# Sparse attention in pairs of heads, the convolution norm under the query columns, and conv units of w_out in one PSUM region

## The chip, the cores and the metric

The kernel runs on one core of a Trainium2 chip. The metric is the device time of one execution in microseconds.

## What is computed

Two transformer blocks in float32 over 256 tokens of width 2048. The change touches the first block's mixer: native sparse attention (16 query heads of 64, 4 key/value heads; three branches: compressed blocks, selected blocks, window) beside a conformer convolution, both closed by one projection `w_out`. With 256 tokens the selection takes all four blocks and the window reaches everything, so those two branches are causal attention over all keys.

```python
proj = rms_norm(x, mix_norm_g) @ w_in                    # q, kv, gate_logits, conv_in
# per query head: three causal softmaxes
p_cmp = masked_softmax(q_s @ k_cmp.T + bias_c, valid_c)  # 15 compressed keys
p_sel = masked_softmax(q_s @ k_slc.T + bias_s, valid_s)  # 256 keys
p_win = masked_softmax(q_s @ k_win.T + bias_w, valid_w)  # 256 keys
attn = g0 * (p_cmp @ v_cmp) + g1 * (p_sel @ v_slc) + g2 * (p_win @ v_win)
# convolution branch
u = causal_depthwise_conv(a * sigmoid(gate), conv_w, conv_b)
conv = silu(layer_norm(u, conv_ln_g, conv_ln_b))
x = x + concatenate([attn, conv], -1) @ w_out
```

Behind it come a gated FFN with convolution, then a second block (latent attention and differential attention, gated mix, FFN) and a final norm.

## The kernel before, in words

Activations lie transposed, features on partitions and the 256 tokens in the free dimension. Each large product splits its operands in a high part (fp32r) and a low remainder: `hp`/`yp` hold for each k-tile 256 high and 256 low columns, and each weight tile is brought by SP's queue into `w_raw`, rounded by ScalarE into `w_hi` (`hi`, L531) and its remainder made by GpSimd (until the q columns) or VectorE in `w_lo` (`lo`, L849). Four slots of such weight units rotate. `unit` (L1507 to L1520) is the matmul form: per k-tile one matmul of `w_hi` with 512 columns (high and low of the activation, into the two halves of a PSUM bank) and one of `w_lo` with the 256 high columns; the two halves are added by VectorE when it takes the bank.

The order of work on every engine is written out by hand and tied together with semaphores. `free` waits until VectorE has taken so many chunks, `used` until PE has finished so many units.

After the q columns of w_in (four groups g, each four units, taken by VectorE at L865) the stage of the change begins:

- The convolution's layer norm. PE sums `conv_y` after q group 0 and its squares after q group 2 (`sums`, L1592). VectorE centres it (L1120), forms the variance (L1128), and after the last q group refines the root (L976 to L979), scales (L1130) and applies gain and bias (L1132, eight ops). ScalarE makes the root and a sigmoid (L644); VectorE gates (L1186), ScalarE copies the high half (L676), VectorE makes the low half (L1190, "mixed").
- Attention, head by head. PE: `scores(h)` (L1712 to L1716, 64 partitions as contraction, the head's half of the array's rows), into banks 2+2s and 3+2s with s = h % 3. VectorE: `scores` (L1147 bias and scale, L1149 to L1152 maxima). ScalarE: `exps` (L652). VectorE: `weighted` (L1159 to L1163, one over the sum times the gate, applied to all segments). PE: `turns` (L1505, eight transposes). ScalarE: `turned` (L659 to L661, copies to ptA, ptB). PE: `values` (L1738 to L1743, 64 output partitions, the head's half of the array's columns, bank 1). Every second head: ScalarE `y_hi` (L666), VectorE `y_lo` (L1169).
- Under it, one conv unit of w_out a head from head 2 on (`conv_unit`): the eight k-tiles of the convolution rows for one 128-column tile of w_out, into bank 0 (the last into bank 4); VectorE's `conv_out` adds the bank's two halves to x (L1176, L1177). Its weights go through `hi` and `lo` like all others.

PE's loop before is, for head h: scores(h+1), turns(h-1), conv_unit(h-2), values(h-1). After the last head the product `w_out` over the attention rows begins (`gemm`).

## Time and profile before

| | before |
|---|---|
| median of 3 runs | 3037.05 us (3034.68 to 3042.62) |
| the profiled execution | 3043.87 us |
| its span | 3041.9 us |
| PE busy | 2947.5 us (97%) |
| DVE busy | 2118.6 us (70%) |
| ACT busy | 1371.4 us (45%) |
| mean granted clock of PE | 0.975 |
| DMA | 507.34 MB, 167 GB/s |

A PE row is one engine pass; an fp32 matmul is two passes with a weight load each. PEld is the weight load, which may overlap PE. The granted clock is in parts of 2.4 GHz (1.0 and 0.5 are its two levels). Times in the views are microseconds from the span's start, and the bracket at a row's end is how long the engine stood idle ahead of it and what ended that.

### The profile page before, as it was taken

The page shows a single profiled execution, that of the slowest core. Times are in us where ns is not written, and L with a number is a line of the kernel's source. Part 1 is how long each engine was busy: PE and PEld are TensorE (multiplying, and loading weights), DVE is VectorE, ACT ScalarE, POOL GpSimd, SP SyncE. Part 2 cuts the span into 40 slices and gives each one's busy share as a digit, 9 for nine tenths or more (in the row PEclk, how much of TensorE's full clock was granted, in tenths as well). Part 3 has the DMA queues.
Part 4 walks back from the last instruction along what each step waited for, and adds up shares of the span by engine and source line. Part 5 has one row for each costly group of instructions (what it writes and reads, how often), then busy time and mean ns, then how long its engine had stood idle before and what let it go on. Part 6 is the DMA issues. An engine that isn't in the chain of part 4 may idle for free.

```text
span 3041.9 us, 49637 instructions
## 1 busy us (share of the span) xinstructions
PE 2947.5 (97%) x16944; PEld 2562.0 (84%) x16944; DVE 2118.6 (70%) x3202; ACT 1371.4 (45%) x1786; POOL 172.4 (6%) x81
## 2 busy tenths in 40 slices
PE   7998999999999999969999999999999999999998
PEld 5877788888888888958878888888888888888887
DVE  4974777885887687557776777777756766675674
ACT  4324555653454455324444455454345543343444
POOL 4864000000000000000000000000000000000000
PEclk9998899999999999889999999999999999999998
DMA  9655135655555565435445655555555655656553
GB/s 229 177 139 120 58 91 166 192 183 190 184 187 188 187 190 166 128 99 143 141 142 182 178 172 165 172 172 174 187 164 175 196 191 184 196 178 201 181 181 123
DMA packets 596729, 507.34 MB, mean 167 GB/s; under 512 B 90123, under 2 KB 594715, under 8 KB 596251
## 3 DMA queue, kind: packets, MB, share of 16 engines
q1 hardware_dynamic: 595040, 503.61, 54.9%
q0 software_dynamic: 560, 2.12, 0.2%
q8 instruction: 53, 0.87, 0.1%
q10 hardware_dynamic: 1035, 0.40, 0.1%
q14 instruction: 41, 0.34, 0.0%
HBM read 503.88 MB, written 2.12 MB: 166 GB/s over the span
## 4 chain that ended last, share of the span: by engine, by line
PE 91%; DVE 6%; issue 1%; ACT 1%; DMA 0%; DVEq 0%; SPq 0%; ACTq 0%
PE banks L1518 55%; PE banks L1519 28%; PE banks L1573 2%; PE banks L1505 1%; DVE arena L865 1%; DVE w_lo L849 1%; DVE banks L1043 1%; PE banks L1592 1%; PE banks L1712 0%; PE banks L1832 0%; DMA cst<-tables 0%; PE banks L1879 0%; PE banks L1738 0%; PE banks L1835 0%; PE banks L1600 0%
## 5 line engine op out<-in xcount | busy, mean ns | idle before, releaser
L1518 PE MATMUL banks<-hp,w_hi 128*128 128x512 f32 x4416 | 1573.8, 400 | 24.3 <-issue 10.0
L531 ACT ACTIVATE w_hi<-w_raw 128x1024 fp32r<-128x1024 f32 (+2 forms) x960 | 996.9, 1045 | 1212.2 <-PE banks L1519 1206.1
L849 DVE TENSOR_TENSOR w_lo<-w_raw,w_hi 128x1024 fp32r<-128x1024 f32 (+2 forms) x889 | 1062.0, 1205 | 565.7 <-ACT w_hi L531 548.6
L1519 PE MATMUL banks<-hp,w_lo 128*128 128x256 f32 x4416 | 1241.9, 281 | 0.0
L1518 PEld LDWEIGHTS banks<-hp,w_hi 128*128 128x128 f32 x4416 | 835.8, 189 | 226.5 <-issue 18.5
L1518 PE MATMUL banks<-yp,w_hi 128*128 128x512 f32 x2880 | 1014.8, 397 | 2.7 <-DVE yp L1267 2.6
L1519 PEld LDWEIGHTS banks<-hp,w_lo 128*128 128x128 f32 x4416 | 840.8, 190 | 2.4 <-issue 1.9
L1519 PE MATMUL banks<-yp,w_lo 128*128 128x256 f32 x2880 | 808.3, 281 | 0.0
L1518 PEld LDWEIGHTS banks<-yp,w_hi 128*128 128x128 f32 x2880 | 543.3, 189 | 128.8 <-DVE yp L1267 3.6
L1519 PEld LDWEIGHTS banks<-yp,w_lo 128*128 128x128 f32 x2880 | 547.1, 190 | 0.1
L865 DVE TENSOR_REDUCE arena<-banks 128x256 f32<-128x512 f32 (+1 forms) x392 | 251.3, 683 | 120.1 <-PE banks L1519 119.8
L834 POOL TENSOR_TENSOR w_lo<-w_raw,w_hi 128x1024 fp32r<-128x1024 f32 x71 | 170.1, 2399 | 82.5 <-ACT w_hi L531 82.2
L1518 PE MATMUL banks<-arena_r,w_hi 128*128 128x512 f32 x272 | 100.0, 407 | 15.4 <-DVE w_lo L849 15.1
L1043 DVE SCALAR_TENSOR_TENSOR banks<-arena,vec,banks 128x256 f32<-128x256 f32 x232 | 102.0, 485 | 3.7
L966 DVE TENSOR_TENSOR arena<-arena,cst 128x512 f32<-128x512 f32 x133 | 91.9, 691 | 4.3
L1239 DVE SCALAR_TENSOR_TENSOR arena<-arena,vec 128x256 f32<-128x256 f32 x176 | 77.5, 481 | 17.1 <-ACT arena L704 11.2
L1519 PE MATMUL banks<-arena_r,w_lo 128*128 128x256 f32 x272 | 77.1, 284 | 0.0
L1518 PEld LDWEIGHTS banks<-arena_r,w_hi 128*128 128x128 f32 x272 | 52.0, 191 | 29.0 <-issue 15.1
L704 ACT ACTIVATE arena<-arena,vec 128x256 f32<-128x256 f32 x88 | 48.2, 595 | 51.2 <-DVE arena L966 51.2
L1212 DVE TENSOR_TENSOR x<-banks,x 128x256 f32<-128x256 f32 (+1 forms) x128 | 53.1, 415 | 20.5 <-PE banks L1519 20.5
L694 ACT ACTIVATE arena<-arena 128x512 f32<-128x512 f32 x44 | 27.8, 633 | 80.6 <-DVE arena L966 61.4
L762 ACT ACTIVATE arena<-arena,small 128x128 f32<-128x128 f32 x64 | 28.7, 449 | 76.9 <-DVE small L1352 76.9
(234 smaller groups left out, 1489.9 us busy)
## 6 DMA issues: line engine op xcount, KB each, us to landing
w_raw<-in_w_in SPq DMA_DIRECT2D x480, 256.0 KB, 3.0
w_raw<-in_w_up SPq DMA_DIRECT2D x352, 256.0 KB, 2.9
w_raw<-in_w_ffn_up SPq DMA_DIRECT2D x176, 256.0 KB, 3.7
w_raw<-in_w_ffn_gate SPq DMA_DIRECT2D x176, 256.0 KB, 3.0
w_raw<-in_w_down SPq DMA_DIRECT2D x160, 256.0 KB, 3.0
w_raw<-in_w_ffn_down SPq DMA_DIRECT2D x160, 256.0 KB, 3.0
w_raw<-in_w_out SPq DMA_DIRECT2D x128, 256.0 KB, 3.2
w_raw<-in_w_mla_proj SPq DMA_DIRECT2D x64, 256.0 KB, 3.0
```

The lines of the kernel that those rows point to most:

```text
L531: nc.scalar.activation(w_hi[:, s, 0:n], w_raw[:, s, 0:n], ACT.Copy).then_inc(hi_ready, 1)
L704: ins = nc.scalar.activation(dst[:, c, :], buf[:, c, FTAPS - 1:], ACT.Identity, scale=vdyn("ffn_conv_w", ch + (FTAPS - 1) * 2 * FT), bias= ...
L834: nc.gpsimd.tensor_tensor(w_lo[:, s, 0:n], w_raw[:, s, 0:n], w_hi[:, s, 0:n].bitcast(f32), ALU.subtract)\
L849: v.tensor_tensor(w_lo[:, s, 0:n], w_raw[:, s, 0:n], w_hi[:, s, 0:n].bitcast(f32), ALU.subtract)\
L865: v.tensor_reduce(dst, pair(b)[0:rows], X, ALU.add).then_inc(chunk_out, 1)
L966: return v.tensor_tensor(dst, dst, bcast(r_row, 2), ALU.mult)
L1043: ins = v.scalar_tensor_tensor(conv_y[:, t, :] if k == TAPS - 1 else acc, src, w, acc, ALU.mult, ALU.add)
L1212: link(v.tensor_tensor(xt, banks[:, c, 0:T], xt, ALU.add))
L1239: ins = v.scalar_tensor_tensor(dst[:, c, :], buf[:, c, k:k + T], vdyn("ffn_conv_w", at_ch[c] + k * 2 * FT), dst[:, c, :], ALU.mult, ALU.add)
L1518: mm(banks[:, b, :], w_hi[:, s, at:at + P], rhs[:, kt, :], start=kt == kt_first, stop=False)
L1519: ins = mm(banks[:, b, 0:T], w_lo[:, s, at:at + P], rhs[:, kt, 0:T], start=False, stop=kt == kt_last)
L1573: ins = mm(banks[:, STAT, at + b:at + b + 1], src[:, t, b * P:(b + 1) * P], ones[:, 0:1], start=False, stop=t == KT - 1, skip_group_check= ...
```

## The change

1. The norm of the convolution: its second sums go after q group 1; VectorE's refinement, scaling and affine follow there, gate and low half behind q group 2; ScalarE's root, sigmoid and high copy are placed between its q high halves.
2. Heads go in pairs. `scores(n)` on PE interleaves the two heads of a pair matmul by matmul (one in array rows 0 to 63, one in 64 to 127); `values(n)` interleaves them too (output partitions 0 to 63 and 64 to 127, both in bank 1). PE's loop is, for pair n: turns(2n), conv_unit(2n), scores(n+1), turns(2n+1), conv_unit(2n+1), values(n). Conv units start with head 0.
3. A conv unit (`folded`) accumulates its three products in one region of 256 columns: per k-tile `w_hi` with the high half, `w_hi` with the low half, `w_lo` with the high half, all 256 columns, in half n % 2 of bank 0. `conv_out` is one add.

```diff
@@ -637,12 +635,15 @@
     nc.scalar.activation(gtok, gtok, ACT.Sigmoid).then_inc(sem("gates_sigmoid"), 1)
     act.wait_ge(sem("conv_centred"), 1)
     nc.scalar.activation(conv_sq, conv_y, ACT.Square).then_inc(sem("conv_squares"), 1)
-    his("q", 0, 8, 16)
+    his("q", 0, 8, 12)
     root(ROOT["conv"], nv_conv)
-    his("w_out_conv", 0, 0, 2)
+    his("q", 0, 12, 14)
     act.wait_ge(sem("conv_affine"), 1)
     nc.scalar.activation(conv_sq, conv_y, ACT.Sigmoid).then_inc(sem("conv_sigmoid"), 1)
-    his("w_out_conv", 0, 2, 4)
+    his("q", 0, 14, 16)
+    act.wait_ge(sem("conv_gated"), 1)
+    nc.scalar.activation(yp[:, CT:KT, 0:T], conv_y, ACT.Copy).then_inc(sem("conv_hi"), 1)
+    his("w_out_conv", 0, 0, 4)
     def exps(h):
@@ -665,22 +666,25 @@
         act.wait_ge(sem("nsa_pv"), n + 1)
         nc.scalar.activation(yp[:, n, 0:T], banks[:, 1, 0:T], ACT.Copy).then_inc(sem("nsa_hi"), 1)
-    for h in range(NQ):
...
+    def next_hi(n):
+        if n < 12:
+            hi("w_out_conv", 0, n + 4)
+        else:
+            hi("w_out", 0, n - 12)
+    exps(0)
+    exps(1)
+    for n in range(NQ // 2):
+        turned(2 * n)
+        next_hi(2 * n)
+        if n:
+            y_hi(n - 1)
+        turned(2 * n + 1)
+        if n < NQ // 2 - 1:
+            exps(2 * n + 2)
+            exps(2 * n + 3)
+        next_hi(2 * n + 1)
     y_hi(NQ // 2 - 1)
-    his("w_out", 0, 2, 4)
     closing("w_out")
     tiny_root(ROOT[1], tiny(0), tiny(1))
@@ -1123,14 +1127,19 @@
             dve.wait_ge(sem("gates_sigmoid"), 1)
             g0 = gtok[:, 0, :].rearrange("p (h r) -> p h r", r=NBR)[:, :, 0]
             link(v.tensor_scalar(g0, g0, c_("sees"), None, ALU.mult))
-        if g == 2:
             dve.wait_ge(sem("conv_sum"), 2)
             v.tensor_scalar(nv_conv[:, 0, :], banks[:, 7, T:], 1.0 / CCH, EPS, ALU.mult, ALU.add).then_inc(sem("variance"), 1)
-    refine(ROOT["conv"], nv_conv)
...
+            refine(ROOT["conv"], nv_conv)
+            link(v.tensor_tensor(conv_y, conv_y, bcast(nv_conv[:, 2, :], CT), ALU.mult))
+            for t in range(CT):
+                ins = v.tensor_scalar(conv_y[:, t, :], conv_y[:, t, :], vcol("conv_ln_g", t), vcol("conv_ln_b", t),
+                                      ALU.mult, ALU.add)
+            ins.then_inc(sem("conv_affine"), 1)
+        if g == 2:
+            dve.wait_ge(sem("conv_sigmoid"), 1)
+            v.tensor_tensor(conv_y, conv_y, conv_sq, ALU.mult).then_inc(sem("conv_gated"), 1)
+            dve.wait_ge(sem("conv_hi"), 1)
+            v.tensor_tensor(yp[:, CT:KT, T:], conv_y, yp[:, CT:KT, 0:T].bitcast(f32), ALU.subtract).then_inc(sem("mixed"), 1)
     def scores(h):
@@ -1172,38 +1181,34 @@
     def conv_out(n):
         used("w_out_conv", 0, n + 1)
-        b = CONV_BANK.get(n, 0)
...
+        v.tensor_tensor(x[:, n, :], banks[:, 0, n % 2 * T:(n % 2 + 1) * T], x[:, n, :], ALU.add).then_inc(chunk_out, 1)
+    def next_lo(n):
+        if n < 12:
+            lo("w_out_conv", 0, n + 4)
+        else:
+            lo("w_out", 0, n - 12)
+    scores(0)
+    scores(1)
+    lows("w_out_conv", 0, 0, 4)
+    weighted(0)
+    weighted(1)
+    for n in range(NQ // 2):
+        conv_out(2 * n)
+        if n < NQ // 2 - 1:
+            scores(2 * n + 2)
+            scores(2 * n + 3)
+        if n:
+            y_lo(n - 1)
+        next_lo(2 * n)
+        if n < NQ // 2 - 1:
+            weighted(2 * n + 2)
+        conv_out(2 * n + 1)
+        next_lo(2 * n + 1)
+        if n < NQ // 2 - 1:
+            weighted(2 * n + 3)
+    y_lo(NQ // 2 - 1)
     def residual(c0):
         def run(i):
@@ -1504,6 +1509,17 @@
         return nc.tensor.transpose(dst, src, ident[0:rows, 0:rows])
+    def folded(ph, j, k0, ku, o, rhs, kt_last):
+        s, r = slot_of(ph, j)
+        pe.wait_ge(lo_ready[s], r + 2)
+        for k in range(ku):
+            kt, wh, wl = k0 + k, w_hi[:, s, k * P:(k + 1) * P], w_lo[:, s, k * P:(k + 1) * P]
+            mm(o, wh, rhs[:, kt, 0:T], start=k == 0, stop=False)
+            mm(o, wh, rhs[:, kt, T:], start=False, stop=False)
+            ins = mm(o, wl, rhs[:, kt, 0:T], start=False, stop=kt == kt_last)
+        ins.then_inc(unit_used, 1)
     def unit(ph, i, j, k0, ku, cols, where, rhs, kt_last, operand=None, kt_first=0):
@@ -1697,23 +1713,26 @@
             ins.then_inc(sem("gates_turned"), 1)
             pe.wait_ge(sem("conv_done"), 1)
             sums(banks[:, 7, 0:T], conv_y, CT).then_inc(sem("conv_sum"), 1)
-        if g == 2:
+        if g == 1:
             pe.wait_ge(sem("conv_squares"), 1)
             sums(banks[:, 7, T:], conv_sq, CT).then_inc(sem("conv_sum"), 1)
-    def scores(h):
...
+    def scores(n):
+        pr = n // GRP
+        if n:
+            pe.wait_ge(sem("nsa_pt"), 2 * n - 1)
+        heads = [(slice(a * HD, (a + 1) * HD), 2 + 2 * ((2 * n + a) % 3)) for a in range(2)]
         for br in range(2):
-            mm(banks[:, 2 + 2 * s, br * T:(br + 1) * T], q1, kvT[r, 1 + br, 0, pr, :], start=True, stop=True)
...
+            for r, b in heads:
+                mm(banks[:, b, br * T:(br + 1) * T], qT[r, n, P:T], kvT[r, 1 + br, 0, pr, :], start=True, stop=True)
+            for r, b in heads:
+                mm(banks[:, b + 1, br * P:(br + 1) * P], qT[r, n, 0:P], kvT[r, 1 + br, 0, pr, 0:P], start=True, stop=True)
+        kc = kcm[:, pr * NCMP:(pr + 1) * NCMP]
+        for r, b in heads:
+            mm(banks[:, b + 1, 256:256 + NCMP], qT[r, n, P:T], kc[r], start=True, stop=True)
+        for r, b in heads:
+            mm(banks[:, b + 1, 272:272 + NCMP0], qT[r, n, 0:P], kc[r, 0:NCMP0], start=True, stop=True).then_inc(sem("nsa_scores"), 1)
     def turns(h):
@@ -1726,31 +1745,27 @@
         turn(banks[0:NCMP0, 3 + 2 * s, 256:384], e[:, 784:784 + NCMP0])
         turn(banks[0:NCMP, 3 + 2 * s, 384:512], e[:, 768:768 + NCMP]).then_inc(sem("nsa_turned"), 1)
-    def values(h):
...
+    def values(n):
+        pr = n // GRP
+        pe.wait_ge(sem("nsa_pt"), 2 * n + 2)
+        if n:
             pe.wait_ge(sem("nsa_lo"), n)
-        pa, pb = ptA[h % 2], ptB[h % 2]
...
+        for j in range(6):
+            for a in range(2):
+                r = slice(a * HD, (a + 1) * HD)
+                o, pa, pb = banks[r, 1, 0:T], ptA[a], ptB[a]
+                dst, vt, pt = ((o, vtm[:, 0, 0, pr, r], pa[:, 0:T]), (o, vtm[:, 1, 0, pr, r], pa[:, T:2 * T]),
+                               (o[:, P:T], vtm[:, 0, 1, pr, r], pb[:, 0:P]), (o[:, P:T], vtm[:, 1, 1, pr, r], pb[:, P:T]),
+                               (o[:, 0:P], vcm[0:NCMP0, pr, r], pb[0:NCMP0, 256:384]),
+                               (o[:, P:T], vcm[0:NCMP, pr, r], pb[0:NCMP, 384:512]))[j]
+                ins = mm(dst, vt, pt, start=j == 0, stop=j == 5, skip_group_check=True)
+        ins.then_inc(sem("nsa_pv"), 1)
     def conv_unit(n):
-        if n in CONV_BANK:
...
+        free("w_out_conv", 0, n)
+        folded("w_out_conv", n, CT, 8, banks[:, 0, n % 2 * T:(n % 2 + 1) * T], yp, KT - 1)
     free("q", 0, 8)
     pe.wait_ge(sem("v_tok"), 2)
@@ -1758,19 +1773,15 @@
     pe.wait_ge(sem("gates_tok"), 1)
     pe.wait_ge(sem("variance"), ROOT["conv"])
     scores(0)
-    for h in range(NQ):
...
+    pe.wait_ge(sem("mixed"), 1)
+    for n in range(NQ // 2):
+        turns(2 * n)
+        conv_unit(2 * n)
+        if n < NQ // 2 - 1:
+            scores(n + 1)
+        turns(2 * n + 1)
+        conv_unit(2 * n + 1)
+        values(n)
     pe.wait_ge(sem("nsa_lo"), NQ // 2)
     gemm("w_out", yp, CT, lambda u: None)
```

What this does to the order, first on PE, in the middle of the stage. Before, one head: the end of a head's values, the next head's scores, transposes, the first matmuls of the unit (hp_f holds the softmax tiles, arena q, k and v).

```order
1265 L1743 MATMUL banks<-hp_f,arena 64x128
1266 L1712 MATMUL banks<-arena 128x256
1267 L1713 MATMUL banks<-arena 128x128
1268 L1712 MATMUL banks<-arena 128x256
1269 L1713 MATMUL banks<-arena 128x128
1270 L1715 MATMUL banks<-arena 128x15
1271 L1716 MATMUL banks<-arena 128x7
1272 L1505 MATMUL banks<-cst,hp_f 128x128 x6
1273 L1505 MATMUL banks<-cst,hp_f 7x128
1274 L1505 MATMUL banks<-cst,hp_f 15x128
1275 L1518 MATMUL banks<-yp,w_hi 128x512
1276 L1519 MATMUL banks<-yp,w_lo 128x256
```

Now, one pair: the end of unit 2n, the next pair's scores, the transposes of head 2n+1, ahead of unit 2n+1 and, behind it, the values of pair n.

```order
1240 L1520 MATMUL banks<-yp,w_lo 128x256
1241 L1728 MATMUL banks<-arena 128x256 x2
1242 L1730 MATMUL banks<-arena 128x128 x2
1243 L1728 MATMUL banks<-arena 128x256 x2
1244 L1730 MATMUL banks<-arena 128x128 x2
1245 L1733 MATMUL banks<-arena 128x15 x2
1246 L1735 MATMUL banks<-arena 128x7 x2
1247 L1510 MATMUL banks<-cst,hp_f 128x128 x6
1248 L1510 MATMUL banks<-cst,hp_f 7x128
1249 L1510 MATMUL banks<-cst,hp_f 15x128
...
1274 L1762 MATMUL banks<-hp_f,arena 64x256 x4
1275 L1762 MATMUL banks<-hp_f,arena 64x128 x8
```

Two heads' scores now stand together, and so do their values; a unit stands on each side of the scores.

VectorE in the middle of the stage (x<-banks is conv_out, w_lo the low half of a weight unit, RECIPROCAL begins `weighted`). Before, one head:

```order
309 L1147 SCALAR_TENSOR_TENSOR hp_f<-banks,arena 128x512
...
316 L1152 TENSOR_REDUCE small<-hp_f 128x1
317 L1176 TENSOR_TENSOR x<-banks,x 128x256
318 L1177 TENSOR_TENSOR x<-banks,x 128x256
319 L1159 RECIPROCAL small<-small 128x6
...
325 L849 TENSOR_TENSOR w_lo<-w_raw,w_hi 128x1024
326 L1147 SCALAR_TENSOR_TENSOR hp_f<-banks,arena 128x512
```

Now, between one pair's conv_out and the first weighting of the next pair:

```order
174 L1184 TENSOR_TENSOR x<-banks,x 128x256
175 L1156 SCALAR_TENSOR_TENSOR hp_f<-banks,arena 128x512
...
182 L1161 TENSOR_REDUCE small<-hp_f 128x1
183 L1156 SCALAR_TENSOR_TENSOR hp_f<-banks,arena 128x512
...
190 L1161 TENSOR_REDUCE small<-hp_f 128x1
191 L1178 TENSOR_TENSOR yp<-banks,yp 128x256
192 L853 TENSOR_TENSOR w_lo<-w_raw,w_hi 128x1024
193 L1168 RECIPROCAL small<-small 128x6
```

Both heads' scores, y's low half and a low half of a weight now lie between conv_out and the weighting; before, one head's scores and conv_out.

VectorE at the start of the stage. Before, from the last variance to the first scores:

```order
103 L1128 TENSOR_SCALAR yp_f<-banks 128x256
104 L865 TENSOR_REDUCE arena<-banks 128x256 x2
105 L976 RECIPROCAL yp_f<-yp_f 128x256
106 L977 TENSOR_TENSOR yp_f<-yp_f 128x256
107 L978 SCALAR_TENSOR_TENSOR yp_f<-yp_f 128x256
108 L979 SCALAR_TENSOR_TENSOR yp_f<-yp_f 128x256
109 L1130 TENSOR_TENSOR arena<-arena,yp_f 128x8x256
110 L1132 TENSOR_SCALAR arena<-arena,vec 128x256 x8
111 L1147 SCALAR_TENSOR_TENSOR hp_f<-banks,arena 128x512
```

Now:

```order
100 L869 TENSOR_REDUCE arena<-banks 128x256 x2
101 L1129 TENSOR_SCALAR arena<-arena,cst 128x16
102 L1131 TENSOR_SCALAR yp_f<-banks 128x256
103 L980 RECIPROCAL yp_f<-yp_f 128x256
...
107 L1133 TENSOR_TENSOR arena<-arena,yp_f 128x8x256
108 L1135 TENSOR_SCALAR arena<-arena,vec 128x256 x8
109 L869 TENSOR_REDUCE arena<-banks 128x256 x2
110 L1140 TENSOR_TENSOR arena<-arena,yp_f 128x8x256
111 L1142 TENSOR_TENSOR yp<-arena,yp 128x8x256
112 L869 TENSOR_REDUCE arena<-banks 128x256 x2
113 L1156 SCALAR_TENSOR_TENSOR hp_f<-banks,arena 128x512
```

The last q take (L865, L869) stood ahead of the norm and now stands behind it and behind the gate and the low half.

## Rows read from the trace of the kernel before

**Rows 1.** Windows: busy us (instructions) of PE, PEld, DVE, ACT, POOL; then PE clock, DMA.

```profile
300.00:320.00 20.00, 9.95 (x35) 7.55 (x36) 13.04 (x37) 8.96 (x35) 0.00 (x0) 0.50 0.27 80
340.00:360.00 20.00, 20.00 (x125) 16.11 (x125) 15.50 (x50) 12.76 (x47) 0.00 (x0) 1.00 0.19 55
```

**Rows 2.** Timeline of PE, the start of the stage: start, us, instruction, [idle before].

```profile
285.68 0.70 PE L1712 MATMUL banks<-arena 64*128 64x256 f32 x2 [1.38 <-DVE arena L865]
...
288.60 1.06 PE L1712 MATMUL banks<-arena 64*128 64x256 f32 x2
...
291.33 1.06 PE L1712 MATMUL banks<-arena 64*128 64x256 f32 x2
...
308.85 1.97 PE L1505 MATMUL banks<-cst,hp_f 128*128 128x128 f32 x8 [15.38 <-DVE hp_f L1163]
```

**Rows 3.** Timeline of DVE, the start of the stage.

```profile
269.86 1.29 DVE L865 TENSOR_REDUCE arena<-banks 128x256 f32<-128x512 f32 x2 [9.80 <-PE banks L1519]
...
284.34 1.29 DVE L865 TENSOR_REDUCE arena<-banks 128x256 f32<-128x512 f32 x2 [10.67 <-PE banks L1519]
285.55 1.74 DVE L976 RECIPROCAL yp_f<-yp_f 128x256 f32<-128x256 f32 x1
...
293.62 1.17 DVE L1147 SCALAR_TENSOR_TENSOR hp_f<-banks,arena 128x512 f32<-128x512 f32 x4
...
295.89 2.35 DVE L849 TENSOR_TENSOR w_lo<-w_raw,w_hi 128x1024 fp32r<-128x1024 f32 x2
298.15 2.28 DVE L1186 TENSOR_TENSOR arena<-arena,yp_f 128x2048 f32<-128x2048 f32 x1
```

**Rows 4.** Timeline of PE, one head of the steady part.

```profile
348.66 0.65 PE L1738 MATMUL banks<-hp_f,arena 128*64 128x256 f32 x2
...
350.68 0.70 PE L1712 MATMUL banks<-arena 64*128 64x256 f32 x2
...
352.53 1.09 PE L1505 MATMUL banks<-cst,hp_f 128*128 128x128 f32 x8
353.38 0.47 PE L1518 MATMUL banks<-yp,w_hi 128*128 128x512 f32 x1
...
356.33 0.65 PE L1738 MATMUL banks<-hp_f,arena 128*64 128x256 f32 x2
```

**Rows 5.** Timeline of DVE, steady part.

```profile
329.41 0.42 DVE L1169 TENSOR_TENSOR yp<-banks,yp 128x256 fp32r<-128x256 f32 x1
329.75 1.17 DVE L1147 SCALAR_TENSOR_TENSOR hp_f<-banks,arena 128x512 f32<-128x512 f32 x4
...
333.38 0.42 DVE L1176 TENSOR_TENSOR x<-banks,x 128x256 f32<-128x256 f32 x1 [1.28 <-PE banks L1519]
...
334.18 0.18 DVE L1159 RECIPROCAL small<-small 128x6 f32<-128x6 f32 x1
...
335.79 1.22 DVE L849 TENSOR_TENSOR w_lo<-w_raw,w_hi 128x1024 fp32r<-128x1024 f32 x1
```

**Rows 6.** Timelines of PE and DVE, the end of the stage.

```profile
432.05 0.51 PE L1518 MATMUL banks<-yp,w_hi 128*128 128x512 f32 x1
...
434.98 0.40 PE L1518 MATMUL banks<-yp,w_hi 128*128 128x512 f32 x1
...
432.57 0.43 DVE L1169 TENSOR_TENSOR yp<-banks,yp 128x256 fp32r<-128x256 f32 x1 [1.56 <-ACT yp L666]
```

**Rows 7.** Timeline of PE, latent attention: two 64-row halves.

```profile
1378.07 0.70 PE L1835 MATMUL banks<-arena 64*128 64x256 f32 x4
```

**Rows 8.** Windows after two gaps of PE, and the timeline rows that end the gaps.

```profile
225.50:229.00 3.50, 3.50 (x13) 3.02 (x12) 3.33 (x8) 0.59 (x1) 0.12 (x1) 0.51 0.92 199
2953.50:2957.00 3.50, 2.52 (x14) 2.14 (x14) 3.43 (x5) 0.84 (x1) 0.00 (x0) 1.00 0.05 13
...
224.06 0.50 PE L1518 MATMUL banks<-hp,w_hi 128*128 128x512 f32 x1 [2.05 <-DVE arena L1063]
...
2954.55 0.50 PE L1518 MATMUL banks<-hp,w_hi 128*128 128x512 f32 x1 [0.98 <-DVE hp L1285]
```

More of the change, by code:

```diff
@@ L72 @@
 NCST = _n
-UNIT0 = 2
-CONV_BANK = {15: 4}
 PARTS = [(0, 16), (16, 16), (32, 12)]
@@ L1174, in conv_out @@
                 used("w_out_conv", 0, n + 1)
-                b = CONV_BANK.get(n, 0)
-                link(v.tensor_tensor(x[:, n, :], banks[:, b, 0:T], x[:, n, :], ALU.add))
-                v.tensor_tensor(x[:, n, :], banks[:, b, T:], x[:, n, :], ALU.add).then_inc(chunk_out, 1)
-            for h in range(NQ):
-                scores(h)
-                if h >= UNIT0 + 1:
-                    conv_out(h - UNIT0 - 1)
-                if h == 0:
-                    lows("w_out_conv", 0, 0, 2)
-                    dve.wait_ge(sem("conv_sigmoid"), 1)
-                    v.tensor_tensor(conv_y, conv_y, conv_sq, ALU.mult).then_inc(sem("conv_gated"), 1)
-                    lows("w_out_conv", 0, 2, 4)
-                if h == 1:
-                    dve.wait_ge(sem("conv_hi"), 1)
-                    v.tensor_tensor(yp[:, CT:KT, T:], conv_y, yp[:, CT:KT, 0:T].bitcast(f32), ALU.subtract).then_inc(sem("mixed"), 1)
-                if h >= 1:
-                    weighted(h - 1)
-                if UNIT0 < h <= UNIT0 + 12:
-                    lo("w_out_conv", 0, h - UNIT0 + 3)
-                elif h > UNIT0 + 12:
-                    lo("w_out", 0, h - UNIT0 - 13)
-                if h >= 3 and h % 2:
-                    y_lo((h - 3) // 2)
@@ L1199, in _ @@
-            weighted(NQ - 1)
-            conv_out(13)
-            lo("w_out", 0, 1)
-            conv_out(14)
-            y_lo(7)
-            lo("w_out", 0, 2)
-            conv_out(15)
-            lo("w_out", 0, 3)
+                v.tensor_tensor(x[:, n, :], banks[:, 0, n % 2 * T:(n % 2 + 1) * T], x[:, n, :], ALU.add).then_inc(chunk_out, 1)
[4 more added lines that the diff above has]
+                    lo("w_out", 0, n - 12)
@@ L1747, in conv_unit @@
-            def conv_unit(n):
-                if n in CONV_BANK:
-                    pe.wait_ge(sem("nsa_pt"), NQ - 2)
-                else:
-                    free("w_out_conv", 0, n)
-                unit("w_out_conv", 0, n, CT, 8, P, (CONV_BANK.get(n, 0),), yp, KT - 1, (sem("mixed"), 1), CT)
+            def values(n):
+                pr = n // GRP
+                pe.wait_ge(sem("nsa_pt"), 2 * n + 2)
+                if n:
+                    pe.wait_ge(sem("nsa_lo"), n)
+                for j in range(6):
[8 more added lines that the diff above has]
+                ins.then_inc(sem("nsa_pv"), 1)
@@ L1760, in _ @@
             scores(0)
-            for h in range(NQ):
-                if h < NQ - 1:
-                    scores(h + 1)
-                if h >= 1:
-                    turns(h - 1)
-                if h >= UNIT0:
-                    conv_unit(h - UNIT0)
-                if h >= 1:
-                    values(h - 1)
-            turns(NQ - 1)
-            conv_unit(14)
-            values(NQ - 1)
-            conv_unit(15)
+            pe.wait_ge(sem("mixed"), 1)
[7 more added lines that the diff above has]
+                values(n)
             pe.wait_ge(sem("nsa_lo"), NQ // 2)
```

39 lines of the change are left out of this document (removed).

## The prediction

> **What bounds the kernel now.** I read the page first. Matmuls fill nearly the whole span and the chain of waits lies on PE almost everywhere, so a change can pay only where PE stands still, runs at half clock, or has less to do. The change touches one place: from the end of the q columns (PE's first score at 285.68 us) to the first w_out tile at 434.98 [rows 2, 6]. The windows of that place show two regimes: between 300 and 320 PE is busy half the time at a granted clock of 0.50, between 340 and 360 all the time at 1.00 [rows 1].
>
> PE's timeline shows where the first regime comes from: after three heads' scores PE stands 15.38 us until the transposes of 308.85, released by DVE [rows 2]. DVE's timeline says what DVE does meanwhile: from 285.55 the conv norm's root refinement, scaling and affine (8.07 us), then softmax work, four low halves, and 2 x 2.28 us of gating and splitting the conv output [rows 3]. Ahead of that DVE stood 9.80 us and 10.67 us waiting for q columns [rows 3].
>
> In the second regime a head costs PE 7.67 us (348.66 to 356.33): values 2.02, scores 1.85, transposes 0.85, conv unit 2.95 [rows 4]. DVE does one head in the same 7.7 us with slack: scores 2.27 (293.62 to 295.89), two conv adds 0.80, weighting 1.61, low half 1.13 (2.26 for two), and every second head 0.34 for the low half of y [rows 3, 5]. PE bounds it.
>
> **The change, part by part.** Times are on the profiled execution's axis until the last step.
>
> *Conv norm under the q columns.* The second sums (eight matmuls) go one q column group earlier; PE has the same work and no new wait. DVE's 8.07 us and its 4.6 us of gate and split move into its idle stretches, with ScalarE's root, sigmoid and copy between them. Starting after the q take of about 260 the chain is some 3.6 (sums) + 0.7 (root) + 8.1 + 2 (sigmoid) + 2.3 + 2 (copy) + 2.3 = 21 us, near 281, before the last q take at 284.34 [rows 3]. I cost it at nothing; the cover is the q matmuls, and if it overran, the scores would start later one for one. q's last two high halves now queue behind the sigmoid on ScalarE, but about two units ahead of their matmuls.
>
> *Start.* PE scores one pair, at half clock about one cold head (288.60 to 291.33, 2.73 [rows 2]), so DVE starts at 288.4: two scores 4.54, four low halves 4.52, one weighting 1.7 with its end. First transposes at 299.2 instead of 308.85. They and the first conv unit start cold: 1.7 to 2.0 for the transposes, and for the unit I take 4.2, between the warm 2.95 [rows 4] and its double, 5.9.
>
> *Scores in pairs.* In the trace two 64-row halves do run together: at 1378.07 four passes of two halves take 0.70 us, and at 350.68 two passes of one half take 0.70 [rows 4, 7]. A pair's scores cost 1.85, not 3.70.
>
> *Values in pairs.* These share all 128 rows and halve the columns; no row of before has two column halves in flight. Bounds: 2.02 (as the row halves do) and 4.04 (two heads after each other [rows 4]). I take 2.02, because the row halves are the nearest case. The Trainium skill (TensorE: Matmul & The Clock Gate, "What overlaps and what doesn't" and the speedup table) measured column tiles almost as quick as row tiles. Both ends give nearly one total, as the next step shows.
>
> *Folded conv units.* Three 256-column matmuls a k-tile for one of 512 and one of 256: the same columns and eight more weight loads. I keep 2.95. Eight transposes with their own loads run in 0.85, 0.11 each [rows 4], so a load fits behind a 256-column matmul. The DVE adds of a unit fall from 0.80 to 0.40.
>
> *The new cycle.* It is set by waits, not by the sum of an engine. The rows of the changed order put, per pair, on PE: transposes, unit, next pair's scores, transposes, unit, values. On DVE both heads' scores, y's low half and a weight's low half now stand between the score matmuls and the weighting that releases the next transposes. From one pair's first transposes to the next: 0.85 + 2.95 + scores with signal 2.0 [rows 4], then 4.54 + 0.34 + 1.2 + 1.7 + 0.1 for DVE [rows 3, 5]: 13.65 us, against 15.34 for two heads now. PE's own work is 1.70 + 5.90 + 1.85 + 2.02 = 11.47, so PE idles about 2.2 us each pair, behind the values. DVE is now what PE waits for. If the values don't overlap, PE's 13.5 still fits. ScalarE's exponentials of the second head end about 2 us before their weighting. conv_out(2n) now gates the second unit, but DVE is free then.
>
> *Sum.* First transposes 299.2; first cycle 2.0 + 4.2 + 2.0 + 7.5 = 15.7, to 314.9; six cycles of 13.65 = 81.9, to 396.8; last pair 0.85 + 2.95 + 0.85 + 2.95 + 2.02 = 9.6, to 406.4; y's halves 1.0 (432.05 to the end of 432.57 [rows 6]), so w_out starts at 407.4 instead of 434.98: 27.5 us earlier.
>
> *The clock.* The new 2.2 us gaps have a price. After a gap of 2.05 us at 222.0 the granted clock of 225.5 to 229 was 0.51; after one of 0.98 at 2953.6 it stayed 1.00 [rows 8]. One such stretch of 3.5 us costs 1.7 us, on the loop (transposes and unit follow the gap). Between none and two stretches in each of seven pairs that is 0 to 24 us. Half-array matmuls alone did not cost the clock (340 to 360 is full of them, at 1.00 [rows 1]). I take one stretch in four pairs of seven, 7 us. Saving: **20.7 us**.
>
> The stages behind are PE-bound and start earlier by as much. The profiled execution took 3043.87 us (span 3041.9), which becomes 3023.2. It lay 6.8 above the median of the three runs, so on that median the forecast is 3037.05 - 20.7 = **3016.3 us**.
>
> **The rivals.**
> - *Column halves don't overlap.* PE is busy 13.5 of 13.65 us, no gap and no fall of clock; only the last pair pays 2.0. Saving 25.5, 3011.5 us. For it: no row shows such a pair, and both would stream different data into the same rows. Against: the row halves, with other weights and other data in each, do [rows 7].
> - *Clock falls in every pair, for two stretches.* 27.5 - 24 = 3.5 saved, 3033.5. For it: the clock of 300 to 320 is 0.50 though PE resumed transposes, values and scores at 308.85 [rows 1, 2]. Against: each pair has two full-array units that should bring it back.
> - *Exposed weight loads in the folded unit.* Then a unit costs 24 x 0.107 more than its 2.6 us of columns, 5.2 instead of 2.95. On the loop 7 x 2.3 = 16, the second unit hidden in the gap, first and last pair some 7: saving 4.5, 3032.5. By the Trainium skill (same page, "What overlaps and what doesn't") a weight load overlaps running matmuls only if its row group differs, which is this case; the 16 matmuls of a unit already run in 2.95 us with all their loads, where their 6,144 columns alone need 2.6 [rows 4], which speaks against it; the trace does not agree with the rule so far.
> - *Slower.* The clock stays at half over transposes, unit and scores of every pair: their 5.65 us double, 7 x 5.65 = 39.6 against 27.5, +12, 3049 us. It decides from 3.9 us of loop work at half clock per pair on. The gap sits just ahead of the transposes, which ran cold for long after 308.85; but the clock is 1.00 again in 340 to 360, where full-array units run between the same half-array work [rows 1].
> - *Not what it says:* the norm overruns the q columns by as much as it saves, or w_out's weights are not there at 407. q's gap with DVE idle (20.5 us in two takes) speaks against the first, four weight slots filled a unit ahead against the second. If half the norm stayed exposed (some 6 us), 15 of the saving would be left, 3022.
>
> **Chances.** Forecast 0.52, column halves serial 0.23, norm or weights late 0.06; these are faster, and so is a little of the exposed loads. Clock in every pair 0.07, exposed loads 0.06, slower 0.06. What a measurement of this kernel can tell from no change is about 0.3%, 9.1 us. That gives faster 0.83, the same 0.11, slower 0.06. The range: at the fast end no clock fall, a warm first unit and a little less per folded unit, 29 us saved, 3008; at the slow end six saved, which reaches through most of the clock's bounds, 3031.
>
> **What would show it.** In the profile after: (1) DVE's norm work between about 262 and 281, and the q columns' end still near 284.3. (2) First transposes at 299, not 309. (3) Score rows of 64 x 128 in near-simultaneous twos, and a pair's scores about 1.85 us. (4) Values of a pair 2.0 us, or 4.0 in the rival. (5) From a pair's first transposes to the next's 13.65 us, DVE idle below 20% there, and PE's wait ahead of the transposes released by DVE's weighting, 2.2 us. (6) The granted clock's mean from 310 to 407: 1.00 without falls, near 0.9 with four. (7) A folded unit 2.95. (8) w_out's first matmul near 407 plus the clock's 7. I am wrong if the cycle is 11.5 (DVE doesn't bind), if it is over 15.3, or if w_out starts early and the end doesn't move with it.

## The result, and the profile after

The changed kernel takes 3018.05 us (median of five executions, 3011.09 to 3023.26) against 3037.05 before; the ratio is 0.9929, with a 95% interval of 0.9908 to 0.9950. The ratio is that of the means of five executions each and stands for 21.6 us less, 15 to 28; the medians differ by 19.0. The forecast was 3016.3 us, 20.7 less.

The page of the profiled execution (3011.09 us, the fastest of the five; that of before, 3043.87 us, was slower than each of the five that its median is from):

```profile
span 3009.3 us, 49899 instructions
PE 2905.0 (97%) x17072; PEld 2535.5 (84%) x17072; DVE 2115.3 (70%) x3186; ACT 1371.2 (46%) x1786; POOL 177.3 (6%) x81
```

The start of the stage on PE, for [rows 2]; the same columns:

```profile
289.99 0.70 PE L1728 MATMUL banks<-arena 64*128 64x256 f32 x4 [1.38 <-DVE arena L869]
...
302.88 1.94 PE L1510 MATMUL banks<-cst,hp_f 128*128 128x128 f32 x8 [10.96 <-DVE hp_f L1172]
```

The 15.38 us gap is now 10.96. But the first scores start at 289.99, not 285.68: in the q columns ahead of them is a new gap of 3.15 us, and from 281.1 to 285 the granted clock is 0.57. PE and GpSimd there, and DVE for [rows 3]:

```profile
281.13 0.62 PE L1534 MATMUL banks<-hp,w_hi 128*128 128x512 f32 x1 [3.15 <-POOL w_lo L838]
```

```profile
265.35 2.42 POOL L838 TENSOR_TENSOR w_lo<-w_raw,w_hi 128x1024 fp32r<-128x1024 f32 x1 [3.61 <-ACT w_hi L529]
268.12 4.05 POOL L838 TENSOR_TENSOR w_lo<-w_raw,w_hi 128x1024 fp32r<-128x1024 f32 x1 [0.35 <-ACT w_hi L529]
277.56 7.90 POOL L838 TENSOR_TENSOR w_lo<-w_raw,w_hi 128x1024 fp32r<-128x1024 f32 x2 [5.39 <-ACT w_hi L529]
```

```profile
265.52 4.39 DVE L1133 TENSOR_TENSOR arena<-arena,yp_f 128x2048 f32<-128x2048 f32 x1
269.95 4.64 DVE L1135 TENSOR_SCALAR arena<-arena,vec 128x256 f32<-128x256 f32 x8
...
276.57 2.29 DVE L1140 TENSOR_TENSOR arena<-arena,yp_f 128x2048 f32<-128x2048 f32 x1 [0.79 <-ACT yp_f L642]
280.84 2.38 DVE L1142 TENSOR_TENSOR yp<-arena,yp 128x2048 fp32r<-128x2048 f32 x1 [1.98 <-ACT yp L645]
288.65 1.29 DVE L869 TENSOR_REDUCE arena<-banks 128x256 f32<-128x512 f32 x2 [5.43 <-PE banks L1535]
```

DVE's scaling of `conv_y` takes 4.39 us and its eight affine ops 4.64. In the kernel before, where GpSimd had ended its last subtraction at 273.3, the same ops took 2.29 and 2.67:

```profile
288.70 2.29 DVE L1130 TENSOR_TENSOR arena<-arena,yp_f 128x2048 f32<-128x2048 f32 x1
291.03 2.67 DVE L1132 TENSOR_SCALAR arena<-arena,vec 128x256 f32<-128x256 f32 x8
```

GpSimd is slower too: one subtraction took 4.05 us and two took 7.90, where the one of 265.35 took 2.42. PE waits 3.15 us for the second last low half of the q columns.

The steady part on PE, one pair, for [rows 4], and on DVE, for [rows 5]:

```profile
344.93 2.10 PE L1762 MATMUL banks<-hp_f,arena 128*64 128x256 f32 x24 [1.26 <-DVE yp L1178]
...
351.47 0.70 PE L1728 MATMUL banks<-arena 64*128 64x256 f32 x4
...
358.54 2.10 PE L1762 MATMUL banks<-hp_f,arena 128*64 128x256 f32 x24 [1.26 <-DVE yp L1178]
```

```profile
344.37 0.41 DVE L1178 TENSOR_TENSOR yp<-banks,yp 128x256 fp32r<-128x256 f32 x1
344.69 1.21 DVE L853 TENSOR_TENSOR w_lo<-w_raw,w_hi 128x1024 fp32r<-128x1024 f32 x1
345.83 0.18 DVE L1168 RECIPROCAL small<-small 128x6 f32<-128x6 f32 x1
...
353.43 1.18 DVE L1156 SCALAR_TENSOR_TENSOR hp_f<-banks,arena 128x512 f32<-128x512 f32 x4 [1.43 <-PE banks L1735]
...
355.71 1.17 DVE L1156 SCALAR_TENSOR_TENSOR hp_f<-banks,arena 128x512 f32<-128x512 f32 x4
...
357.98 0.41 DVE L1178 TENSOR_TENSOR yp<-banks,yp 128x256 fp32r<-128x256 f32 x1
```

A pair takes 358.54 - 344.93 = 13.61 us. The scores of both heads start together (L1728 x4 in the 0.70 us of x2 before), and the values of two heads with 24 passes take about 2.1 us. PE's idle time is in two pieces: 1.26 us ahead of the values, released by DVE's L1178 (`y_lo`), and about 0.5 ahead of the transposes, by the weighting. The waits of the steady part, total us, count and longest:

```profile
PE banks L1762 <- DVE yp L1178: 7.6, 6, 1.3
...
PE banks L1510 <- DVE hp_f L1172: 2.7, 5, 0.5
```

The windows for [rows 1] (the first 1.2 cycles, then to the end of the stage); the columns as there:

```profile
302.90:322.30 19.40, 17.85 (x129) 16.45 (x130) 12.18 (x43) 10.12 (x35) 0.00 (x0) 0.76 0.32 87
322.30:413.00 90.70, 78.66 (x745) 71.36 (x743) 70.70 (x229) 59.40 (x205) 0.00 (x0) 1.00 0.29 81
```

From 322.3 on PE is idle 12 of 90.7 us, and the clock is 1.00 throughout. The stage ends with this row, for [rows 6]:

```profile
413.03 0.49 PE L1534 MATMUL banks<-yp,w_hi 128*128 128x512 f32 x1 [1.23 <-DVE yp L1178]
```

w_out starts at 413.03 instead of 434.98, 21.95 us earlier. The spans differ by 32.6. The other 10.7 us lie behind the stage, in code that the change doesn't touch. The rest from w_out on took 2606.9 us in the profile of before and 2596.3 in that of after; in the profiles of the experiments it lay between 2594.9 and 2611.9. Most of these 10.7 us is clock. The whole rest, before and after:

```profile
434.98:3041.90 2606.92, 2561.10 (x14594) 2235.92 (x14592) 1824.69 (x2508) 1190.09 (x1412) 0.00 (x0) 0.98 0.56 172
413.03:3009.30 2596.27, 2550.60 (x14592) 2226.67 (x14592) 1822.29 (x2505) 1189.01 (x1411) 0.00 (x0) 0.99 0.56 173
```

PE is idle for the same time in both (45.8 and 45.7 us) and busy 10.5 us longer in the first, with the same matmuls. The time lost to the lower clock (1.00 less the granted clock, times the length, added up over windows of 10 us) is an estimated 46 us in the rest of before and 36 in that of after. These two profiles are extremes, and the 10.7 us are no gain of the change: the medians and the means (19.0 and 21.6 us) differ by about what the stage shows. So I read each experiment first by where w_out starts and what a cycle takes, and by the time second.

### The profile page after: what moved, and what is told of

It is laid out like the page before. It is cut to its first block, busy times and chain, and to the rows that moved or that the text cites. A ratio compares the mean times of both kernels' runs of the same rounds, so it can differ in the third digit from the quotient of the medians.

```text
span 3009.3 us, 49899 instructions
## 1 busy us (share of the span) xinstructions
PE 2905.0 (97%) x17072; PEld 2535.5 (84%) x17072; DVE 2115.3 (70%) x3186; ACT 1371.2 (46%) x1786; POOL 177.3 (6%) x81
## 4 chain that ended last, share of the span: by engine, by line
PE 89%; DVE 8%; issue 1%; ACT 1%; DMA 0%; POOL 0%; DVEq 0%; SPq 0%; ACTq 0%
PE banks L1534 54%; PE banks L1535 28%; DVE arena L869 1%; PE banks L1589 1%; DVE w_lo L853 1%; PE banks L1510 1%; DVE banks L1047 1%; DVE hp_f L1156 1%; PE banks L1608 1%; PE banks L1843 0%; DVE small L1158 0%; DMA cst<-tables 0%; PE banks L1890 0%; DVE hp_f L1172 0%; PE banks L1518 0%
## 5 line engine op out<-in xcount | busy, mean ns | idle before, releaser
L1534 PEld LDWEIGHTS banks<-hp,w_hi 128*128 128x128 f32 x4416 | 835.7, 189 | 230.9 <-issue 18.4
L1534 PE MATMUL banks<-yp,w_hi 128*128 128x512 f32 x2752 | 963.8, 395 | 3.9 <-DVE yp L1272 2.6
L1535 PE MATMUL banks<-yp,w_lo 128*128 128x256 f32 x2752 | 771.5, 280 | 0.0
L1534 PEld LDWEIGHTS banks<-yp,w_hi 128*128 128x128 f32 x2752 | 517.6, 188 | 122.7 <-DVE yp L1272 3.6
L1535 PEld LDWEIGHTS banks<-yp,w_lo 128*128 128x128 f32 x2752 | 521.7, 190 | 0.1
L869 DVE TENSOR_REDUCE arena<-banks 128x256 f32<-128x512 f32 (+1 forms) x392 | 251.3, 683 | 105.0 <-PE banks L1535 104.6
```

The lines of the kernel that those rows point to most:

```text
L869: v.tensor_reduce(dst, pair(b)[0:rows], X, ALU.add).then_inc(chunk_out, 1)
L1534: mm(banks[:, b, :], w_hi[:, s, at:at + P], rhs[:, kt, :], start=kt == kt_first, stop=False)
L1535: ins = mm(banks[:, b, 0:T], w_lo[:, s, at:at + P], rhs[:, kt, 0:T], start=False, stop=kt == kt_last)
```

## The experiments

Each experiment's ratio is to executions of the kernel before that were taken together with it (their median was 3042.84 us for experiments 1 to 4, 3038.46 for 5 to 8, 3042.90 for 9 to 11), so ratios can be compared across rows and medians only roughly.

| run | q columns end, first scores | first transposes | cycle of a pair | w_out starts | median us | ratio to before |
|---|---|---|---|---|---|---|
| before | 285.68 | 308.85 | 15.3 (2 x 7.67) | 434.98 | 3037.05 | |
| changed | 289.99 | 302.88 | 13.61 | 413.03 | 3018.05 | 0.9929 [0.9908, 0.9950] |
| norm only | 290.84 | 303.64 | 15.3 | 429.2 | 3034.45 | 0.9973 [0.9958, 0.9988] |
| pairs only | 285.17 | 308.44 | 13.62 | 416.6 | 3021.20 | 0.9936 [0.9916, 0.9957] |
| values serial | 289.69 | 302.58 | 14.98 | 420.4 | 3028.68 | 0.9963 [0.9948, 0.9979] |
| scores serial | 290.21 | 303.11 | 13.62 | 411.4 | 3015.23 | 0.9916 [0.9887, 0.9944] |
| q first | 288.71 | 303.27 | 13.62 | 411.0 | 3016.07 | 0.9923 [0.9906, 0.9941] |
| y early | 290.10 | 302.99 | 13.28 | 412.6 | 3017.67 | 0.9930 [0.9914, 0.9947] |
| unit in halves | 289.18 | 302.07 | 13.57 | 409.7 | 3011.50 | 0.9912 [0.9886, 0.9937] |
| weighted sooner | 289.69 | 304.24 | 12.48 | 404.8 | 3009.64 | 0.9895 [0.9876, 0.9915] |
| q lows on DVE | 285.00 | 297.89 | 13.62 | 406.0 | 3016.32 | 0.9919 [0.9901, 0.9937] |
| both | 284.76 | 297.66 | 12.48 | 398.4 | 3008.12 | 0.9884 [0.9869, 0.9899] |
| both, halves | 286.10 | 298.99 | 12.4 | 401.2 | 3007.65 | 0.9890 [0.9875, 0.9904] |

**1. The norm alone.** The kernel before with the norm's hunks of the diff (ScalarE, DVE, PE's sums) and DVE's four low halves together.

```diff
-            his("q", 0, 8, 16)
+            his("q", 0, 8, 12)
...
-                if g == 2:
+                if g == 1:
                     pe.wait_ge(sem("conv_squares"), 1)
```

> The kernel before with the first part alone: the convolution norm under the q columns; attention stays head by head, units in two halves of a bank. Theory (parts are separate): the q columns end near 290 us instead of 285.7, because GpSimd's last two low halves come late, the first transposes start at about 303 instead of 308.9, and from there a head costs 7.7 us as before, so w_out starts near 429 and the time is 6 us below the kernel before, 3031. Rival (most of the changed kernel's 22 us comes from the norm, because the cold stretch goes): w_out starts before 420 and the time is below 3025.

First transposes at 303.64, w_out at 429.2: the theory's numbers. The norm is worth 5.8 of the 22 us. By the ratio the time is about 8 us shorter (4 to 13), where 6 were expected.

**2. The pairs alone.** The changed kernel with those hunks taken back; gate and low half of the norm stand between the first scores again.

```diff
-                if g == 1:
+                if g == 2:
                     pe.wait_ge(sem("conv_squares"), 1)
```

> The changed kernel with the norm back behind the last q group: pairs and folded units alone. Theory: the q columns end at 285.7, the first transposes start at 309 after a gap of 20 us, then cycles of 13.6 us a pair; w_out starts near 419, the time is 16 us below the kernel before, 3021. Rival (norm is most of it): w_out near 430 and 3031.

```profile
308.44 1.94 PE L1509 MATMUL banks<-cst,hp_f 128*128 128x128 f32 x8 [21.34 <-DVE hp_f L1166]
```

w_out at 416.6, 18.4 us earlier than before and 2.4 earlier than expected: 0.6 is the start, and against the changed kernel the first cycle takes 0.5 less and the second 1.6 less (13.62 us, not 15.20), where the clock didn't fall. The clock is up again in the first unit (0.97 from 313 to 316), while in the kernel before it was 0.50 until 323. The parts alone give 5.8 + 18.4 = 24.2, together 21.95; most of the difference is the same fall in the changed kernel's second pair.

**3. Values head after head.**

```diff
-                for j in range(6):
-                    for a in range(2):
+                for a in range(2):
+                    for j in range(6):
```

> The changed kernel with the values of a pair issued head after head, so that column halves no longer meet. The prediction on record said that this fits into the wait of PE: only the last pair pays 2 us, w_out near 415. Theory formed from the trace after: values(n) waits for the low half of y of the pair before, which stands on DVE behind both heads' scores, so the values start 10.9 us into a cycle of 13.6 and 4.0 us of them overrun it: cycle 15.0 us, w_out near 425, the time 11 to 12 us above the changed kernel.

```profile
343.50 4.08 PE L1762 MATMUL banks<-hp_f,arena 128*64 128x256 f32 x24 [1.26 <-DVE yp L1178]
...
358.48 4.08 PE L1762 MATMUL banks<-hp_f,arena 128*64 128x256 f32 x24 [1.26 <-DVE yp L1178]
```

The values take 4.08 us instead of 2.10, and the cycle is 14.98 us. Column halves do overlap, with different data in the same rows, and that is worth 1.4 us a pair. The time is about 10.3 us longer (the ratios differ by 0.0034; their intervals just touch); the stage shows 7.4 of it (420.4 against 413.0). "PE's 13.5 still fits", in the prediction, is refuted.

**4. Scores head after head.** The loop over the two heads outside, both branches inside it.

```diff
-                for br in range(2):
-                    for r, b in heads:
+                for r, b in heads:
+                    for br in range(2):
```

> The changed kernel with the scores of a pair issued head after head. If the 1.85 us of PE time that the pairing saves lie on the cycle: 15.3 us a cycle and 12 us above the changed kernel. Theory: DVE can start on the first head's scores after the same 1.9 us, and works 2.3 us on them while PE does the second head, so the cycle stays at 13.6 us (PE's gap ahead of the values goes instead) and the time is that of the changed kernel within 2 us.

Cycle 13.62 us and w_out at 411.4: pairing the scores gains no time. PE's idle time takes what the scores cost more: none is left ahead of the values and 0.47 us ahead of the transposes. That w_out is even 1.6 us earlier is the clock, which did not fall in the second pair; there the gap was 0.37 us instead of 1.55.

**5. The q high halves ahead of the sigmoid.**

```diff
-            his("q", 0, 12, 14)
+            his("q", 0, 12, 16)
...
-            his("q", 0, 14, 16)
```

> The changed kernel with ScalarE's last two high halves of the q columns ahead of the norm's sigmoid instead of behind it. Theory (the q columns end late because these two wait for DVE's affine): the 3.15 us gap of PE at 278 and the half-clock stretch behind it go, first scores at 285.7 to 286.5 instead of 290.0, time 4 to 5 us below the changed kernel. Rival (GpSimd and DVE slow each other down while both run, the low halves come late anyway): the gap shrinks to 1.5 to 3 us and the time falls by less than 2.

The theory fails, and the rival's mechanism shows in another place than it said. The gap inside the q columns went, but a gap of 4.64 us stands ahead of the first scores, because DVE is later still; w_out starts only 2.0 us earlier:

```profile
265.65 4.42 DVE L1132 TENSOR_TENSOR arena<-arena,yp_f 128x2048 f32<-128x2048 f32 x1
270.11 8.81 DVE L1134 TENSOR_SCALAR arena<-arena,vec 128x256 f32<-128x256 f32 x8
```

```profile
265.52 2.40 POOL L837 TENSOR_TENSOR w_lo<-w_raw,w_hi 128x1024 fp32r<-128x1024 f32 x1 [3.44 <-ACT w_hi L529]
268.35 8.80 POOL L837 TENSOR_TENSOR w_lo<-w_raw,w_hi 128x1024 fp32r<-128x1024 f32 x3 [0.43 <-ACT w_hi L529]
```

With GpSimd at work without a pause, the same eight affine ops take 8.81 us. They are not all slow: the first three, at 270.11, 272.40 and 274.81, take 2.37, 2.50 and 2.48 us, and each ends 0.14 to 0.16 us after one of GpSimd's subtractions; the other five take about 0.33 us each. In the changed kernel it is the first alone, 2.38 us at 269.95. So an op of one engine stands until the other's op has ended; experiment 9 tests it by taking GpSimd away.

**6. y early.** DVE's `y_lo(n - 1)` ahead of conv_out, ScalarE's `y_hi(n - 1)` ahead of the copies.

```diff
+                if n:
+                    y_lo(n - 1)
                 conv_out(2 * n)
...
                     scores(2 * n + 3)
-                if n:
-                    y_lo(n - 1)
```

> The changed kernel with the low half of y ahead of conv_out and the scores on DVE (and its high half ahead of the transposed copies on ScalarE). Values no longer wait. Theory: the cycle shrinks by DVE's 0.34 to 13.3 us, and PE's idle time is one gap of 2 us ahead of the transposes instead of 1.26 us ahead of the values and 0.6 behind them; then the granted clock falls in some pairs, 1.7 us each, which was the clock term of the prediction: w_out between 411 and 420. Rival (a gap of 2 us a pair does not cost the clock): no half-clock stretch between 322 and 400, w_out at 410.5.

The steady cycle is 13.28, and the idle time is one gap of 1.54 us ahead of each pair's transposes. At two of the seven gaps the clock fell behind it, at 318.78 and at 373.50, and the cycles there took 14.87 and 14.84:

```profile
373.50 1.97 PE L1510 MATMUL banks<-cst,hp_f 128*128 128x128 f32 x8 [1.54 <-DVE hp_f L1172]
```

```profile
342.00:372.00 30.00, 26.87 (x260) 23.74 (x258) 25.58 (x85) 21.97 (x85) 0.00 (x0) 1.00 0.25 71
372.00:378.00 6.00, 4.50 (x25) 4.35 (x26) 4.84 (x18) 3.55 (x11) 0.00 (x0) 0.72 0.41 124
```

So the clock's price, 1.6 us each, exists where the gap is in one piece, but not every time: two falls cost 3.2 us where the changed kernel pays for one, and w_out starts only 0.4 us earlier although the cycle is 0.33 us shorter.

**7. Units in halves.** `unit` with 512 and 256 columns instead of `folded`, and two adds.

```diff
-                folded("w_out_conv", n, CT, 8, banks[:, 0, n % 2 * T:(n % 2 + 1) * T], yp, KT - 1)
+                unit("w_out_conv", 0, n, CT, 8, P, (0,), yp, KT - 1, None, CT)
```

> The changed kernel with conv units as before: one 512-column and one 256-column matmul a k-tile into both halves of the bank, and two adds on DVE. Theory: the unit takes the same 2.95 to 3.05 us on PE and the second add (0.4 us a unit) falls into DVE's slack, so cycle 13.6 to 13.7 us and time equal within 2 us. Rival (DVE is what bounds the cycle, so 0.8 us a pair more on it lengthens it): cycle 14.4 us, 6 us above the changed kernel.

Cycle 13.57 us: the third part of the change gains nothing. A folded unit is a little longer (348.43 to 351.47, 3.04 us, against 2.95 in [rows 4]), and the add it saves lay in DVE's slack. That w_out is 3.4 us earlier than in the changed kernel comes from the start (0.8), the first cycle (0.8) and the second pair, where the clock didn't fall (1.6); the intervals of the two ratios overlap widely.

**8. The first head's weighting directly behind the scores.** With 5's and 6's edits, against which the diff is written. Both low halves of weights also go behind the second add, and one behind the second head's weighting.

```diff
                     scores(2 * n + 3)
+                    weighted(2 * n + 2)
+                conv_out(2 * n + 1)
                 next_lo(2 * n)
                 if n < NQ // 2 - 1:
-                    weighted(2 * n + 2)
-                conv_out(2 * n + 1)
-                next_lo(2 * n + 1)
-                if n < NQ // 2 - 1:
                     weighted(2 * n + 3)
+                next_lo(2 * n + 1)
```

> The changed kernel with the q halves as in the run above (ahead of the sigmoid), the low half of y early, and on DVE the weighting of a pair's first head directly behind the two scores, the weights' low halves behind it. Theory (the cycle is PE's transposes, unit and scores plus DVE's chain to the first weighting): 0.34 and 1.13 us leave the chain, 0.2 us of waiting for the exponentials come in: cycle 12.3 to 12.5 us, w_out near 400, time 12 to 14 us below the changed kernel, 3005. Rival (something else bounds, ScalarE's exponentials or the conv adds): cycle over 13.2 us and under 6 us of gain.

```profile
343.47 1.09 PE L1508 MATMUL banks<-cst,hp_f 128*128 128x128 f32 x8 [0.73 <-DVE hp_f L1171]
...
355.94 1.09 PE L1508 MATMUL banks<-cst,hp_f 128*128 128x128 f32 x8 [0.73 <-DVE hp_f L1171]
```

A cycle of 12.47 us: what stands on DVE between the scores and the first weighting is what bounds the cycle. Of the 1.5 us taken off it 1.1 show; 0.23 is a wait for the exponentials that is new on DVE. w_out is at 404.8 instead of 400 because 5's edit brought its late first scores with it (first transposes at 304.24).

**9. The last four q low halves on DVE.** GpSimd stops after unit 11. ScalarE also makes one more high half ahead of the sigmoid; experiment 5, which makes two more there, kept the slow DVE ops, so that isn't what removes them.

```diff
-            his("q", 0, 12, 14)
+            his("q", 0, 12, 15)
...
-            his("q", 0, 14, 16)
+            his("q", 0, 15, 16)
...
-                for j in range(3 if ph == "conv" else 0, UPS[ph]):
+                for j in range(3 if ph == "conv" else 0, 12 if ph == "q" else UPS[ph]):
...
                     ins.then_inc(sem("conv_affine"), 1)
+                    lows("q", 0, 12, 14)
                 if g == 2:
+                    lows("q", 0, 14, 16)
```

> The changed kernel with the low halves of the last four q units on DVE instead of GpSimd (two behind the norm's affine, two ahead of the gate), and ScalarE's q high halves 12 to 14 ahead of the sigmoid. Theory (DVE's norm ops under the q columns took 4.4 and 4.6 us, and 4.4 and 8.8 in the run with early high halves, instead of 2.3 and 2.7, only because GpSimd subtracts at the same time): with GpSimd silent they take 2.3 and 2.7 again, though DVE has 4.5 us more to do; the 3.15 us gap at 278 and the half clock behind it go, first scores at 285.7 to 286, first transposes at 299, w_out 4 us earlier than 413. Rival (these ops are slow there for another reason, PE's or ScalarE's reads): they stay above 4 us and the first scores come at 288 or later.

```profile
265.19 2.29 DVE L1133 TENSOR_TENSOR arena<-arena,yp_f 128x2048 f32<-128x2048 f32 x1
267.52 2.67 DVE L1135 TENSOR_SCALAR arena<-arena,vec 128x256 f32<-128x256 f32 x8
270.11 2.36 DVE L853 TENSOR_TENSOR w_lo<-w_raw,w_hi 128x1024 fp32r<-128x1024 f32 x2
...
283.65 1.29 DVE L869 TENSOR_REDUCE arena<-banks 128x256 f32<-128x512 f32 x2 [1.09 <-PE banks L1537]
```

2.29 and 2.67 us, though DVE has four low halves more. First scores at 285.00, w_out 7.0 us earlier, where 4 were expected: 5.0 from the start, 0.5 from the first cycle, and 1.6 because the clock didn't fall in the second pair. The rival is out. The time itself, 0.9919 against 0.9929, can't show 7 us with these intervals.

**10. 9 and 8 together.** ScalarE's q high halves as in 9, y early and DVE's order as in 8.

> The run above joined with the order of DVE in which the first head's weighting follows the scores directly. Theory: both gains add, first transposes at 299, cycle 12.5 us, w_out at 400; 3001 to 3005 us and a ratio to the kernel before of 0.987 to 0.989. Rival (the gains are spent on something shared): w_out later than 404.

w_out at 398.4, 14.6 us ahead of the changed kernel; 3008.12 us, 0.9884 [0.9869, 0.9899]. The start of w_out and the ratio are the ones expected, the time in us a few over, and its profile had the longest rest of all (2611.9 us). It beats the kernel before, and its interval lies apart from the changed kernel's.

**11. 10 with units in halves.**

> The run above with conv units as in the kernel before (512 and 256 columns, two adds). Theory: a unit is 0.05 to 0.09 us shorter on PE than the folded one and the second add costs 0.4 us of DVE's slack; with the cycle now 12.5 us, DVE's slack is only about 1.5 us a pair, so the cycle is 12.4 to 12.9 us. Rival: no slack is left and the cycle is 13.3 us.

Cycle 12.3 to 12.5 us, so the slack is enough here too. Time and interval are those of 10, though w_out starts 2.8 us later (1.3 from the start, the rest in the first cycle and the last pair).

## Why the prediction was right

The time, its sign and the cause held: the cycle of waits came out as it was built. That the number is as close as it is (w_out within 1.2 us of its forecast) is luck, since two errors of 4 to 5 us cancelled.

- *Conv norm, costed at nothing: wrong.* That it overruns the q columns was named among the rivals, though by as much as it saves; it cost 4.3 us. I counted DVE's chain (from the refinement on 16.7 us of the 21; measured 20.9, from 262.35 to 283.2) and ScalarE's order, but took DVE's durations from a place where GpSimd stood still [rows 3], and moved the work beside GpSimd's low halves. Experiments 5 and 9 show the size: 4.39 + 4.64 against 2.29 + 2.67. The Trainium skill has the rule (SBUF — State Buffer, "SBUF: two separate sides"): DVE and GpSimd share a pair of ports, and when a DVE op has two SBUF inputs or uses a two-port mode, whichever engine starts first holds the pair for its whole instruction while the other waits. The trace agrees: GpSimd's subtraction of 265.35 keeps its 2.42 us, the scaling that starts 0.17 us behind it ends 2.14 us after it, and takes 4.39; DVE's product of 276.57 starts first and keeps its 2.29 us. The two subtractions of 277.56 start 1.0 us into this product and 0.2 us into DVE's op of 280.84, and each ends about 2.2 us after that op, at 281.1 and 285.5. I had not weighed it.
- *Start.* From first scores to first transposes 12.9 us (13.5 expected). The first unit took 4.9 from its first matmul to the next scores (304.47 to 309.36), 4.2 assumed.
- *Scores in pairs: the price right, and worth nothing.* 1.85 us, as priced; but DVE can start on the first head as early either way (4). The prediction named no gain for it beyond the cycle and did not see that the cycle was free of it.
- *Values in pairs: taken right, the other end mis-judged.* The step "if the values don't overlap, PE's 13.5 still fits" left out a wait: values(n) needs `y_lo(n-1)`, which DVE does behind both scores. The diff (`nsa_lo` ahead of the values) and the order rows showed it. With 4.08 us the cycle is 14.98 (3), and the rival would have taken about 3029, not 3011.5.
- *Folded units: 2.95 expected, 3.04 measured.* No exposed loads. Its saved add lies in slack (7).
- *The cycle: 13.65 expected, 13.61 measured*, bound by the chain it was built from; taking 1.5 us off that chain took 1.1 to 1.2 off the cycle (8, 11). DVE is idle 2.5 us of a cycle (18%), below the 20% named.
- *The gap: 2.2 us ahead of the transposes expected*, measured 1.26 ahead of the values and 0.5 ahead of the transposes: the same missed wait split it.
- *The clock: 7 us assumed for four pairs.* Inside the stage one fall, at the second pair's transposes behind a gap of 1.55 us (their cycle took 15.20), 1.6 us. With one gap a pair it was two in seven (6).

Against the sum: with the clock's 6.8 w_out was to start at 414.2. The first transposes came 3.7 late (4.3 from the norm, 0.6 back from the start), first cycle and last pair took 0.6 more, the six cycles between 5.4 less (83.3 against 81.9 + 6.8), 5.2 of it the clock. That gives 413.1; measured 413.03. Behind the stage no gain was forecast, and the medians show none.

What stays open: what decides when the rest's stretches of lower clock come; its code is the same in all runs, and its length moved by 17 us. Between experiments 9 and 10, which have these two ends, the clock accounts for an estimated 8 of the 17 us (added up as above), and for the others the traces name no cause.
